# A linear-attention scan whose keys enter their decays as logarithms

## The reference

```python
def _hgrn2_gate(z, lb):
    f = lb + (1.0 - lb) * jax.nn.sigmoid(z)
    logf = jnp.log(jnp.maximum(f, F_TINY))
    k = (1.0 - lb) * jax.nn.sigmoid(-z)
    return logf, k
# _hgrn2_scan, per chunk and head: bt is the running sum of logf
    decay = exp(bt[t] - bt[s])            # s <= t, per key channel
    scores = einsum(q, k, decay)          # sum over key channels
    o = scores @ v + (q * exp(bt)) @ state
    state = exp(b_last) * state + (k * exp(b_last - bt)).T @ v
```

## Time and profile before

| | |
|---|---|
| three runs | 3475.27, 3471.65, 3474.61 us |
| the profiled execution | span 3475.4 us (the page gives no time around it) |
| busy | PE 3315.4 us (95%), DVE 2112.2 (61%), ACT 969.1 (28%), POOL 1588.7 (46%) |
| the chain that ended last | PE 86%, DVE 7%, ACT 3%, POOL 2%, issue 2% |
| scans | from 2037 to 2201 us and from 2871 to 3037 us of the span |
| in-projections | PE busy in all of 1830 to 1950 us and of 2690 to 2790 us |

### The profile page before, as it was taken

The page is one execution under the profiler, slowest core; times in us unless marked ns, Lnnn a source line. Parts: engine busy times, 40 slices in busy tenths (PEclk is TensorE's granted clock), DMA queues, the critical chain, the costliest instruction groups (busy, mean ns, idle before and its releaser), DMA issues.

```text
span 3475.4 us, 44870 instructions
## 1 busy us (share of the span) xinstructions
PE 3315.4 (95%) x16138; PEld 2538.4 (73%) x16138; DVE 2112.2 (61%) x3509; ACT 969.1 (28%) x2203; POOL 1588.7 (46%) x1534
## 2 busy tenths in 40 slices
PE   8989999999999999999999988999999987899998
PEld 5665555555557967888888756688888865678887
DVE  7577756544544296555646668478764776656554
ACT  2076211001021174211122264222213244332211
POOL 1054322222235224444454467456645547655654
PEclk9999999999999999999999989999999998999999
DMA  7300223333312201345432200244443200022222
GB/s 254 130 10 7 97 98 120 104 122 114 107 58 73 79 2 37 122 158 170 158 96 85 64 12 11 85 156 158 153 143 99 86 28 18 12 88 88 88 89 79
DMA packets 91129, 317.87 MB, mean 91 GB/s; under 512 B 10816, under 2 KB 13152, under 8 KB 90912
## 3 DMA queue, kind: packets, MB, share of 16 engines
q1 hardware_dynamic: 64224, 218.34, 19.5%
q10 hardware_dynamic: 24768, 90.19, 7.1%
q0 software_dynamic: 1920, 6.49, 0.7%
HBM read 312.88 MB, written 2.10 MB: 91 GB/s over the span
## 4 chain that ended last, share of the span: by engine, by line
PE 86%; DVE 7%; ACT 3%; POOL 2%; issue 2%; DMA 0%; DVEq 0%; ACTq 0%; SPq 0%; POOLq 0%
PE ps L1336 66%; PE ps L1338 4%; PE ps L631 3%; PE ps L1293 2%; PE ps L1006 1%; PE ps L1246 1%; PE ps L992 1%; PE ps L1028 1%; PE ps L1189 1%; DVE arena L2626 1%; PE ps L1231 1%; PE ps L1064 1%; ACT arena L1520 1%; DVE arena L2584 1%; PE ps L1261 1%
## 5 line engine op out<-in xcount | busy, mean ns | idle before, releaser
L1336 PE MATMUL ps<-arena 128*128 128x256 f32 (+1 forms) x3744 | 952.4, 408 | 0.2
L1336 PEld LDWEIGHTS ps<-arena 128*128 128x128 f32 x3744 | 710.8, 190 | 204.9 <-issue 1.7
L2757 POOL TENSOR_TENSOR arena<-ring,arena 128x512 f32<-128x512 f32 (+1 forms) x140 | 182.6, 1304 | 836.8 <-PE ps L1336 836.8
L1336 PE MATMUL ps<-arena,ring 128*128 128x256 f32 (+1 forms) x2032 | 524.9, 410 | 3.1 <-ACT arena L1690 3.1
L1336 PE MATMUL ps<-hbuf,ring 128*128 128x256 f32 (+1 forms) x1824 | 469.4, 407 | 4.2 <-ACT hbuf L1797 1.2
L1336 PEld LDWEIGHTS ps<-arena,ring 128*128 128x128 f32 x2032 | 385.3, 190 | 119.5 <-ACT arena L1690 5.9
L1336 PEld LDWEIGHTS ps<-hbuf,ring 128*128 128x128 f32 x1824 | 345.8, 192 | 113.7 <-ACT hbuf L1797 19.5
L2300 DVE TENSOR_TENSOR arena<-ps,arena 128x256 f32<-128x256 f32 (+1 forms) x192 | 86.1, 449 | 356.7 <-PE ps L1336 235.6
L2187 DVE CUSTOM_DVE_ANT_0 aring<-aring,csil,adab 128x1024 f32<-128x1024 f32 x176 | 261.7, 1508 | 1.8
L2305 DVE SCALAR_TENSOR_TENSOR resid<-ps,mod,resid 128x256 f32<-128x256 f32 (+2 forms) x296 | 137.4, 482 | 185.2 <-PE ps L1336 180.5
L2740 POOL TENSOR_TENSOR arena<-ring 128x512 f32<-128x512 f32 (+1 forms) x140 | 182.1, 1301 | 141.2 <-PE ps L1336 133.6
(11 more groups left out here) (324 smaller groups left out, 5342.3 us busy)
## 6 DMA issues: line engine op xcount, KB each, us to landing
aring<-in_ada ACTq DMA_DIRECT2D x172, 512.0 KB, 4.7
ring<-in_mlp SPq DMA_DIRECT2D x128, 512.0 KB, 3.7
ring<-in_up SPq DMA_DIRECT2D x88, 512.0 KB, 3.3
ring<-in_in SPq DMA_DIRECT2D x56, 512.0 KB, 3.3
ring<-in_down SPq DMA_DIRECT2D x32, 512.0 KB, 3.6
ring<-in_odd_in SPq DMA_DIRECT2D x24, 512.0 KB, 3.3
arena<-in_ada SPq DMA_DIRECT2D x16, 512.0 KB, 13.7
ring<-in_out SPq DMA_DIRECT2D x16, 512.0 KB, 3.3
```

The costliest lines, as they stand in the source:

```text
L1336: return nc.tensor.matmul(ps[:, bank, 0:p.tw], w, x, start=start, stop=stop, skip_group_check=True)
L2757: nc.gpsimd.tensor_tensor(s[3], f0[:, h:2 * h], s[1], ALU.subtract).then_inc(wsum_ready, 1)
```

## The change

The logarithm of the key is made once, in the in-projection, with the same split into high and low part as logf. DVE makes both parts (two more instructions of 128x512 a block in `clamps`; k itself is now held above 2^-120), ACT takes two more logarithms a block, POOL adds them. In the attention DVE forms, after each unit's running sums, one 128x512 sum `log k -+ E` (`sum_keys`). In the scan the key half of a level's exponent is the boundary plus or minus this sum, and so Exp gives the weighted key at once: `weigh_levels` goes, and of `weigh_ends` the multiplication of the keys. The query products of POOL take all four chunks in one instruction, 14 of 64x256 a unit in place of 28 of 64x128. PE waits for `level_decay` (ACT's Exp) where it waited for `level_weighed`.

```diff
@@ ends (ACT)
+                    act.wait_ge(keys_summed, 6 * n + u + 1)
+                    plain, of = ((QF, src), (KF, keys))[d]
+                    nc.scalar.activation(plain[:, d, :].rearrange("p (t k) -> p t k", t=4), of, ACT.Exp)
                     for t in range(4):
-                        nc.scalar.activation(ends[:, d, t * P:(t + 1) * P], src[:, t, :], ACT.Exp, scale=-1.0, bias=e[:, t, 128:129])
+                        if d == 0:
+                            nc.scalar.activation(KF[:, d, t * P:(t + 1) * P], keys[:, t, :], ACT.Exp, bias=e[:, t, 128:129])
+                        else:
+                            nc.scalar.activation(QF[:, d, t * P:(t + 1) * P], src[:, t, :], ACT.Exp, scale=-1.0, bias=e[:, t, 128:129])
@@ logarithm (ACT), and its sum on POOL
+                    nc.scalar.activation(log_key(b), log_key(b), ACT.Ln)
+                    nc.scalar.activation(log_key_low(b), log_key_low(b), ACT.Ln)
                     nc.scalar.activation(LF[:, b, :], LF[:, b, :], ACT.Ln)
...
+                            nc.gpsimd.tensor_tensor(log_key(b), log_key(b), log_key_low(b), ALU.add)
@@ attention (DVE)
+                        if p >= 3 and p % 2:
+                            sum_keys(layer - 2, (p - 3) // 2)
...
+            def sum_keys(n, u):
...
+                nc.vector.tensor_tensor(key_sum(r).rearrange("p (a c k) -> p a c k", a=2, c=2), log_key(r).rearrange("p a (c k) -> p a c k", c=2), e,
+                                        ALU.add if d else ALU.subtract).then_inc(keys_summed, 1)
@@ clamps (DVE)
-                nc.vector.tensor_scalar(KR[:, b, :], KR[:, b, :], OMLB[:, b:b + 1], None, ALU.mult)
+                chain(nc.vector.tensor_scalar(KR[:, b, :], KR[:, b, :], OMLB[:, b:b + 1], KEY_TINY, ALU.mult, ALU.max))
+                key = KR[:, b, :].rearrange("p (a t) -> p a t", a=2)
+                nc.vector.tensor_scalar(log_key_low(b), key, SPLIT, 1.0, ALU.mult, ALU.min)
+                nc.vector.tensor_scalar(log_key(b), key, 1.0 / SPLIT, None, ALU.max)
@@ level_exponents, weigh_ends, weigh_levels (DVE)
+                        if d == 0:
+                            nc.vector.tensor_tensor(w[:, :, 0], bd, k[:, :, 0], ALU.add)
+                            nc.vector.tensor_tensor(w[:, :, 1], x[:, :, 1], bd, ALU.subtract)
+                        else:
+                            nc.vector.tensor_tensor(w[:, :, 0], bd, x[:, :, 0], ALU.subtract)
+                            nc.vector.tensor_tensor(w[:, :, 1], k[:, :, 1], bd, ALU.subtract)
...
-                    nc.vector.tensor_tensor(KF[:, d, :], KF[:, d, :], KR[:, 3 * d + b, :], ALU.mult)
...
-                    for li, m in enumerate(LEVELS):
...
-                        x = nc.vector.tensor_tensor(w, w, k, ALU.mult)
-                    x.then_inc(level_weighed, 1)
@@ queries (POOL)
-                                for half in range(2):
-                                    x = nc.gpsimd.tensor_tensor(dst[rows, half, hx], w[rows, 2 * half:2 * half + 2],
-                                                                q[rows, 2 * half:2 * half + 2], ALU.mult)
+                                x = nc.gpsimd.tensor_tensor(dst[rows, hx], w[rows], q[rows], ALU.mult)
```

More of the change, by code:

```diff
@@ L441, in build, with tail_block, log_key, log_key_low @@
         ONE1 = carve(P)
+        LK45 = carve(2 * S, "p (b t) -> p b t", b=2)
+        AR_TAIL = aring[:, :, :].rearrange("p s d -> p (s d)")[:, 6 * 4 * 129:6 * 4 * 129 + S]
+        def tail_block(half, j):
+            return half[:, 2 * j:2 * j + 2, S:T]
+        def log_key(r):
+            return tail_block(H, r) if r < 4 else LK45[:, r - 4, :].rearrange("p (a t) -> p a t", a=2)
+        def log_key_low(r):
+            return tail_block(X, r) if r < 4 else PB2[:, r - 3, :].rearrange("p (a t) -> p a t", a=2)
+        def key_sum(r):
+            return (csil[:, 1, 0:S], csil[:, 1, S:2 * S], JUNK[:, 0:S], AR_TAIL, LK45[:, 0, :], LK45[:, 1, :])[r]
         consts_in = sem("consts_in")
@@ L1246, in scan @@
                                 mm = nc.tensor.matmul(ps[:, 2 + v % 2, t * P:(t + 1) * P], WL[:, 7 * (1 - d) + li, t * P:(t + 1) * P],
-                                                      level_queries(v)[:, t // 2, t % 2 * P:(t % 2 + 1) * P], start=True, stop=True)
+                                                      level_queries(v)[:, t, :], start=True, stop=True)
                             mm.then_inc(level_ready, 1)
@@ L1840, in end_decays @@
                     src = e[:, :, 1 - d:129 - d]
-                    plain, ends = ((QF, KF), (KF, QF))[d]
+                    keys = key_sum(3 * d + b).rearrange("p (t k) -> p t k", t=4)
                     act.wait_ge(cumulated, 6 * n + u + 1)
-                    nc.scalar.activation(plain[:, d, :].rearrange("p (t k) -> p t k", t=4), src, ACT.Exp)
+                    act.wait_ge(keys_summed, 6 * n + u + 1)
+                    plain, of = ((QF, src), (KF, keys))[d]
+                    nc.scalar.activation(plain[:, d, :].rearrange("p (t k) -> p t k", t=4), of, ACT.Exp)
                     for t in range(4):
-                        nc.scalar.activation(ends[:, d, t * P:(t + 1) * P], src[:, t, :], ACT.Exp, scale=-1.0, bias=e[:, t, 128:129])
+                        if d == 0:
+                            nc.scalar.activation(KF[:, d, t * P:(t + 1) * P], keys[:, t, :], ACT.Exp, bias=e[:, t, 128:129])
+                        else:
+                            nc.scalar.activation(QF[:, d, t * P:(t + 1) * P], src[:, t, :], ACT.Exp, scale=-1.0, bias=e[:, t, 128:129])
                     nc.scalar.activation(ET[:, 3 * d:3 * d + 2], e[:, 1:3, 128], ACT.Exp)
@@ L2574, in level_exponents @@
                     dve.wait_ge(cumulated, 6 * n + u + 1)
+                    dve.wait_ge(keys_summed, 6 * n + u + 1)
+                    keys = key_sum(3 * d + b).rearrange("p (t k) -> p t k", t=4)
                     if u == 1:
```

27 lines of the change are left out of this document (12 added, 15 removed).

## The result

The changed kernel takes 3487.12 us (median of 6 runs, 3486.01 to 3490.78), the kernel before 3475.21 us beside it (6 runs, 3471.65 to 3482.07). The ratio is 1.0034, with a 95% interval of 1.0024 to 1.0044: the change makes the kernel slower, by about 12 us or 0.3%. The forecast was 3462 us, with a chance of 0.09 for slower.

The account below looks back on a forecast made before the run. PE bounds most of the span; in the scan no engine is full and PE, DVE and POOL wait in turn. Terms -12.8 - 13.2 + 12 + 1.5 = -12.5 us gave 3462 us, range 3447 to 3474.

Parts of the forecast that it names:

- Unit 0: First unit of each scan: POOL done 8.9 us earlier, 6.4 us gained a scan, 12.8 in both; bounds 4.8 and 8.9 each.
- Units 1 and 3: In both scans each unit shrinks from 25.8 to 22.5 us: 3.3 us each, 13.2 in all; bounds 1.5 and 4.5 each.
- The in-projection: Layers 2 and 3: added DVE and POOL work costs 6 us a layer, 12 in all; bounds 5 and 18.
- The upper bound: In-projection, DVE: longer clamps meet two more weight sums a turn, 1.9 us, making 4.7 us a layer.
- The POOL term: In-projection, turns 7 to 9: two more POOL additions a turn make PE wait, 3 us a layer, up to 4.5.
- The attention: Six sums a layer on DVE, 0.68 us each, mostly hidden: 0.75 us a layer, 1.5 us in all.
- ACT's logarithms at nothing: In-projection: ACT's two more logarithms a block cost nothing, since ACT idles 609.7 us before its copies of products.
- The slower one: Rival: in-projection waits of about 2.6 us lower PE's clock, costing 2 us more each; +8 us, 3482 us, chance 0.10.
- the in-projection hides its new work: Rival: in-projections lose only 1.2 + 4 us, the attention nothing, the scans give 28; 3452 us, chance 0.24.
- PE is the bound in the scan: Rival: PE's clock falls as before, unit 0 gives 4.8, units 1 and 3 give 1.5 each; 3472 us, chance 0.14.
- The lock for a whole instruction: Rival, scan: DVE and POOL exclude each other for whole instructions, a pair costs 1.04 us; 3469 us, chance 0.10.
- prediction's own signs of being wrong: In-projections grow by less than 2 or more than 9 us each, or a scan shrinks by less than 8 us.

Follow-up runs that it names:

- 28 queries: Changed kernel with one Ln a key block and sums at the attention's end, plus 28 short queries from unit 1 on: 3449.41 us, ratio 0.9927.
- split exponents: Changed kernel with one Ln a key block and late sums; odd units' last four exponents behind merges, ACT's end work before level decays: 3449.00 us.
- one Ln: Changed kernel, but one ScalarE Ln with scale 2^60 makes the key's logarithm, without the added clamps, second Ln and second GpSimd addition: 3460.59 us, ratio 0.9957.

## Why the prediction was wrong

- **Unit 0** came out right in size, 6.0 and 5.7 us for 6.4 (6.1 and 7.1 by the forecast's own cut), and half by luck. The third addition took 1.26 us, the queries 0.8 where 0.7 was forecast. But of POOL's 8.9 us, 3.9 were to come from the longer queries, and with the short ones the changed kernel gives as much there (6.8 and 6.0 us): what gave the time is the removed weighing, which let the addition pass and left POOL undisturbed.
- **Units 1 and 3** is the first step that failed: 5.7 us instead of 13.2, and 4.1 by the forecast's own cut. It said that 10 pairs are contended at 0.87 and 4 exponents run alone. The ten pairs and their price were nearly right (0.98 for four, 0.87 for six), the four that run alone were not. I let POOL start 3 us ahead of DVE; it started at 2084.88, 2.9 us ahead indeed, but it went on to its additions of 128x512 (1.33 us each, at 2097.20 and 2098.61) when its queries were done, and these additions I had left out. So no exponent but the first and last ran alone; the two beside the additions cost 1.4 us each, together 2.1 more than alone, of the 2.5 us by which the exponents ended late (P + 13.5 for P + 11.0, with P the start of the pairs). The wait of PE was to fall below 1 us and was 3.13. The runs with 28 queries and with split exponents took it away and gave 9 to 11 us. With only the short queries put back, all four of these units take 20.7 us where 22.5 was forecast: they give 20.8 us, more than the 13.2, and PE needs less than the 22.4 us that the forecast took for its floor.
- **The in-projection** is the second and larger failed step: 22.0 us instead of 12 (22.8 counted from the clamps on), outside the bounds of 5 to 18. Both its terms were too small, and each alone is beyond its own bound. The clamps were priced as two more meetings with weight sums, 1.9 us a turn, partly given back by the taps, 3 us a layer (at most 4.7). In fact the added clamps brought a whole run of four or five clamps beside POOL, each at 1.4 us, and cost 9.9 and 6.4 us without the second addition. The upper bound had the right mechanism and the wrong count: it should have taken all clamps of the block beside which POOL has an instruction, 4 or 5 x 0.95 us a turn. The POOL term was 3 us a layer, at most 4.5, and measures 5.8 and 5.7 without the clamps. In layer 3 they add up to its 12.1; in layer 2 the changed kernel pays 10.7, since its turn 5 was not hit.
- **The attention**: 0.68 us a sum was the uncontended length; they take 1.00 to 1.11, and the phase lost 5.4 us against 1.5. By the run that moved them they cost 7.6 us in both layers, but with one Ln the same phases lost 2.5 us, and moving the sums gave nothing that can be told from none. How much of the loss is theirs stays open.
- **ACT's logarithms at nothing** was right: with one added Ln the in-projection was as before.
- **The rivals.** The slower one was priced at 3482 us, near the result, but by the clock: in the profile above the lower clock cost 1.7 us in each layer, which spared the next turn a wait at least as long, and the stalls made the rest. So its sign came true by luck and its mechanism only in small part. That the in-projection hides its new work is refuted by the 22.8 us. That PE is the bound in the scan is refuted by the run with the short queries, whose units 1 and 3 are 4.8 to 5.7 us shorter, where that rival gave 1.5. The lock for a whole instruction, 1.04 us a pair, is above the 0.87 to 0.98 us of the exponents. The clamps have one input, and they step at 1.41 us beside additions of 1.27 us: they wait for a whole addition each time. The Trainium skill (SBUF — State Buffer, Who interferes with whom) has a sentence on just these: operations such as `tensor_scalar` can run in a mode with both port pairs, and then whoever issues first holds the shared pair for its whole instruction and the other blocks. The timelines agree: 1.37 to 1.54 us for a clamp of 0.42. I had weighed only the sentence on two-input instructions, in the scan, and not this one, in the stage where it decided.
- **Two sums** are off by little and move nothing. The exponents of unit 1 took 8.7 us before (P + 4.9 to P + 13.6), not 9.1, and the 14 queries at 0.705 us with four times 0.1 are 10.3 us, not 10.4. The prediction's own signs of being wrong both came: the in-projections grew by more than 9 us each, and the first scan shrank by 7.4 us, less than 8.

The common error: I priced contention by counting the instructions that are added. The count that matters is of all instructions, old and new, that now fall beside the other engine's.

## What to carry to other kernels

Work on VectorE beside GpSimd is to be priced at GpSimd's step, not at its own: a clamp of 0.42 us cost 1.4 us here, and it costs the old clamps behind it as well. Before joining two short GpSimd instructions into a long one, look at what VectorE does beside them; if TensorE waits for VectorE there, the long form makes it later (0.60 to 0.87 us a step), and halving GpSimd's count gives nothing. Where an added operation can go to an idle ScalarE with a scale or bias inside one activation, that was worth 26 us here. When profiles differ by a few us, count from the last event ahead of the change: from the span's start the in-projections without clamps and additions scattered by up to 1.6 us, from there by 0.01.

## What the runs showed of the hardware that was not expected

- A VectorE clamp of 128x512 (one input, 0.42 us alone) next to GpSimd additions of 128x512 (1.27 us alone) took 1.37 to 1.54 us, and both engines stepped at 1.41 us for five instructions in a row.
- Two-input VectorE instructions of 128x256 (0.34 us apart alone) stepped at 0.60 to 0.66 us beside GpSimd products of 64x128, at 0.87 to 0.98 beside 64x256, and at 1.40 beside 128x512.
- GpSimd products of 64x256 came 0.78 to 0.83 us apart; of 64x128, 0.46 to 0.49 with little beside them.
- A GpSimd addition of 128x512 (1.27 us alone) took 4.09 to 5.62 us beside a row of two-input VectorE instructions of 128x256 that came 0.34 us apart: there it did not take turns with them one by one.
- After a TensorE wait of 2.2 us the granted clock fell in 6 of 18 cases (0.57 over 4 us in one of them); the fall cost 1.7 us and each time spared the next turn its wait of 2.2 or 3.1 us.
